# Gated-recurrent stage: the diagonal and the levels of block 1 and 2 in one product per chunk, and narrower stationary operands in the other levels

## The chip, the cores and the metric

The kernel runs on one core of a Trainium2 chip. The time is that of one execution on the device in microseconds; the figure for a kernel is the median of its runs.

## The reference, cut to what matters

The program is a small language model of three blocks on 512 tokens with 1024 channels: a layer of two recurrent mixers, a layer with the gated recurrence of this case (HGRN2), and an attention layer, each with a feed-forward part. Only the second layer's mixer is touched. For each of its 8 heads (128 key and 128 value channels) it computes

```python
# per head
S_t = diag(f_t) S_{t-1} + k_t v_t^T      # k_t = 1 - f_t
o_t = S_t^T q_t
# inside a chunk:
diff = G_[..., :, None, :] - G_[..., None, :, :]          # G = cumsum(log f) in the chunk
pair_decay = jnp.exp(jnp.where(incl, diff, -jnp.inf))     # incl: key s <= query l
attn = jnp.einsum("bhld,bhlsd,bhsd->bhls", q_, pair_decay, k_)
o = einsum(qd_, state) + einsum(attn, v_)
```

The decay differs by channel, so `attn[l, s] = sum_d q[l,d] k[s,d] exp(G[l,d] - G[s,d])` is a matrix product only if the exponent is split into a part for the query and a part for the key.

## The kernel before, in words

Every tensor lies with its channels on the 128 partitions and the 512 tokens along the free dimension, in NT = 4 chunks of P = 128. The five engines run programs of their own, in an order written out by hand, and meet at counting semaphores (`wait_ge`, `then_inc`).

TensorE has two kinds of work in this stage. **Projections**: each head needs four projections (forget, q, gate, v) of 8 groups each, so 32 groups; a group is one `k.product` of three matmuls (L190 to L192, high x high, low x high, high x low) of 128 x 512. They are worked one head ahead and serve as filling: `fill(h, n)` issues the groups between two numbers of `slots_first` (first head, which begins with ten groups), `slots_next`, or, in the last head, `slots_last` (there they are the first products of the output projection, "mix"). **The head's own products** are plain f32, which the profile shows as two passes, two loads and two matmuls, for each product; a transpose has one.

`core(h)` is the order of a head on TensorE. First the diagonal: q against k, 128 x 128 for each of four chunks (L1208); of this the vector engine keeps only the diagonal (`diagonal`, L1493). Then the norm of the head before (L1200), filling, the transposes of v, and seven **levels** l = 0 to 6. A level with block size b = 2^l covers the pairs whose key lies in an even block of b tokens and whose query lies in the odd block behind it. `diff` (VectorE, L1435) subtracts from G its value at the end of the even block, `exps` (ScalarE, L1290 and L1291) takes exponentials of the even and the odd half with opposite signs, `factor` (GpSimd, L1400 and L1401) multiplies k into the even and q into the odd half, giving X, and `level` (TensorE, L1195) multiplies each chunk of X (stationary, 128 columns) with its odd blocks (moving, 64 columns). `merge` (VectorE, L1488) writes the wanted entries into the attention tile with a predicated copy, after it has issued the difference of the level four further on. Behind the levels come the transposes of the decayed keys (L1223), one group of filling, the key-value product (L1229) which waits for ScalarE's copy of the turned keys (`turned_keys`, L1313), filling, the output (L1237 and L1242), and the last filling.

X, the differences and their exponentials have R = 4 buffers, so level l of a head takes the place of level l - 4, and level 0 to 3 of the next head are prepared while the levels of this one are worked. On GpSimd, `step` first makes the decayed keys (L1405) and decayed queries (L1409), then the factors of levels 4 to 6 and of 0 to 3 of the next head.

Of the kernel before, what the change touches and what calls it, by code (L numbers as in the profile page):

```python
# [32 lines left out]
_CST = [("ident", P), ("ones", P), ("upper", P), ("causal", P), ("chunkdiag", P), ("levels", P * len(LEVELS)),  # L33
# [1039 lines left out]
def hgrn2(k, weights, half):  # L1073
# [17 lines left out]
    S = sb("c_S", [P, NT - 1, P], F32)  # L1091
    b_f, b_q, b_g, b_v, b_x0, b_x1, b_kv, b_o = k.ps
# [5 lines left out]
     o_done, osb_ready, osq_ready, nrm_done, rs_ready, y_ready, ch_act, ch_dve) = (sem("c_" + s) for s in (  # L1098
         "f_taken q_taken g_taken raw_ready v_turned v_ready f_clamped sig_ready ft_ready logf_ready q_ready gate_ready g_ready "
         "kdf_ready e_ready kd_ready qd_ready tr_done kdt_ready kv_done s_ready diff_ready lexp_ready x_ready lv_done at_done "  # L1100
         "o_done osb_ready osq_ready nrm_done rs_ready y_ready ch_act ch_dve").split())
# [22 lines left out]
    def odd_mask(l):  # L1124
        b = LEVELS[l]
        m = odd(k.c("levels", l * P, (l + 1) * P), l).rearrange("p (a n) b -> p a n b", a=1)
        return m.to_broadcast([P, NT, P // (2 * b), b]).bitcast(U32)

    def x_at(h, l):
        return NL * h + l + 1  # L1130

# [6 lines left out]
    with nc.Block() as block:  # L1138
# [15 lines left out]
        def _(pe):  # L1154
# [47 lines left out]
            def core(h):  # L1202
                if h == 0:
                    project(1, 0, slots_first[0])
                pe.wait_ge(q_ready, h + 1)
                pe.wait_ge(diff_ready, x_at(h, 0))
                for c in range(NT):
                    ins = nc.tensor.matmul(b_x0[:, c * P:(c + 1) * P], kk[:, c * P:(c + 1) * P], q[:, c * P:(c + 1) * P], start=True, stop=True)  # L1208
                ins.then_inc(lv_done, 1)
# [5 lines left out]
                for l in range(NL):  # L1215
                    level(h, l)
                    fill(h, l + 1)
# [7 lines left out]
                fill(h, 8)  # L1225
# [5 lines left out]
                fill(h, 9)  # L1231
                pe.wait_ge(at_done, 8 * h + 8)
# [11 lines left out]
                fill(h, 10)  # L1244
# [10 lines left out]
        def _(act):  # L1255
# [18 lines left out]
            def silu_q(h):  # L1274
                act.wait_ge(q_taken, h + 1)
                if h:
                    act.wait_ge(lv_done, 8 * (h - 1) + 1)
# [45 lines left out]
            def step(h):  # L1323
# [13 lines left out]
                exps(h + 1, 0)  # L1337
                turned_keys(h)
                high(h + 2, 1)
                exps(h + 1, 1)  # L1340
# [42 lines left out]
            for l in range(R):  # L1383
                exps(0, l)
# [7 lines left out]
        def _(pool):  # L1392
            def factor(h, l):
# [3 lines left out]
                if h0 >= 0:  # L1397
                    pool.wait_ge(lv_done, 8 * h0 + l0 + 2)
# [4 lines left out]
            def step(h):  # L1403
# [8 lines left out]
                if h < H - 1:  # L1412
                    for l in range(R):
                        factor(h + 1, l)

            for l in range(R):
                factor(0, l)
# [6 lines left out]
        def _(dve):  # L1424
            ch = Chain(dve, ch_dve)

            def diff(h, l):
# [7 lines left out]
                nc.vector.tensor_tensor(dif[:, l % R, :].rearrange("p (n b) -> p n b", b=2 * b), g, ref, ALU.subtract).then_inc(diff_ready, 1)  # L1435

# [44 lines left out]
            def merge(h, l):  # L1481
                dve.wait_ge(lv_done, 8 * h + l + 2)
                dve.wait_ge(at_done, 8 * h + l + 1)
                if l + R < NL:
                    diff(h, l + R)
                else:
                    nc.vector.memset(tick[:, l + R - NL:l + R + 1 - NL], 0.0)
                nc.vector.copy_predicated(odd_chunks(at[:, :], l), odd_mask(l), odd_chunks(b_x[(l + 1) % 2][:, :], l)).then_inc(at_done, 1)  # L1488
# [20 lines left out]
            def step(h):  # L1509
                diagonal(h)  # L1510
                merge(h, 0)
                if h:
                    out(h - 1)
                merge(h, 1)
# [10 lines left out]
                diff(h + 1, 0)  # L1525
                merge(h, 6)
                for l in range(1, R):
# [34 lines left out]
            for l in range(R):  # L1562
# [1743 lines left out]
def constants():  # L3306
# [8 lines left out]
        "levels": np.concatenate([(s // (2 * b) == l // (2 * b)) & (s // b % 2 == 0) & (l // b % 2 == 1) for b in LEVELS], 1),  # L3315
        "sel": np.repeat(s == np.arange(6)[None, :], P, 1),
# [106 lines left out]
```

## Time and profile before

| | |
|---|---|
| median of 3 runs | 1744.38 us (1744.16 to 1747.76) |
| the profiled execution, its own time | 1746.02 us |
| its span in the profile | 1744.2 us |
| TensorE matmul row busy | 1697.7 us (97%) |
| TensorE weight loads | 1385.7 us (79%) |
| VectorE | 1071.2 us (61%) |
| ScalarE | 851.9 us (49%) |
| GpSimd | 441.4 us (25%) |

The stage of this case lies between about 763 and 1045 us of the span. Matmuls are pipelined: a record starts when its instruction is taken up and its length holds the time through the array, so records overlap, and what one costs is read from the distance of starts. "PEld" is the row of the weight loads, "PE" that of the matmuls. "128*128" is partitions times columns of the stationary operand, "x8" the number of records merged into a line.

### The profile page before, as it was taken

The numbers are of one execution on the slowest core, as the hardware profiler recorded it, in microseconds if no ns is written. First come the engines' busy times: TensorE is split into PE (matmuls) and PEld (weight loads), VectorE is DVE, ScalarE is ACT, GpSimd is POOL, SyncE is SP. The second block draws the span as 40 slices with busy tenths as digits, with TensorE's granted clock in tenths as the row PEclk, the third lists the DMA queues.
The fourth block names the chain that finished last, engine by engine and source line by source line (L and its number), as shares of the span: only waits on it lengthen the run. The fifth ranks groups of instructions, "written<-read, shape, count | busy, mean of one in ns | idle before, by whom it ended". The sixth has DMA issues, their size and how long they took to land. (4 is left out here: it accounts for less than half of the span.)

```text
span 1744.2 us, 23896 instructions
## 1 busy us (share of the span) xinstructions
PE 1697.7 (97%) x8362; PEld 1385.7 (79%) x8362; DVE 1071.2 (61%) x1684; ACT 851.9 (49%) x1459; POOL 441.4 (25%) x341
## 2 busy tenths in 40 slices
PE   9999999999999999999999999999999999999997
PEld 6787888878888878778888887888887876777785
DVE  6637444377666643587777758766664357888353
ACT  6757545354333332466555645433333244455573
POOL 1445444101111110025654630111111003232232
PEclk9999999999999999999999999999999999999999
DMA  5312112223222232311211212222222232121121
GB/s 220 130 46 73 37 38 67 73 79 109 96 96 96 86 97 96 119 49 61 73 61 61 72 50 85 91 97 96 97 88 97 96 108 101 49 86 60 49 73 48
DMA packets 40372, 144.25 MB, mean 83 GB/s; under 512 B 4562, under 2 KB 4818, under 8 KB 39780
## 3 DMA queue, kind: packets, MB, share of 16 engines
q1 hardware_dynamic: 40292, 143.20, 24.2%
q8 instruction: 49, 0.80, 0.2%
q14 instruction: 31, 0.25, 0.0%
HBM read 141.05 MB, written 2.13 MB: 82 GB/s over the span
## 5 line engine op out<-in xcount | busy, mean ns | idle before, releaser
L190 PE MATMUL bank<-u_high,w_high 128*128 128x512 f32 x1556 | 635.5, 408 | 7.8 <-DVE w_low L582 2.0
L192 PE MATMUL bank<-u_high,w_low 128*128 128x512 f32 x1556 | 609.0, 391 | 0.0
L191 PE MATMUL bank<-u_low,w_high 128*128 128x512 f32 x1556 | 607.4, 390 | 0.0
L190 PEld LDWEIGHTS bank<-u_high,w_high 128*128 128x128 f32 x1556 | 293.0, 188 | 78.6 <-issue 18.9
L192 PEld LDWEIGHTS bank<-u_high,w_low 128*128 128x128 f32 x1556 | 292.4, 188 | 63.5
L191 PEld LDWEIGHTS bank<-u_low,w_high 128*128 128x128 f32 x1556 | 293.3, 188 | 57.9 <-issue 4.1
L154 ACT ACTIVATE w_high<-w_ring 128x1024 fp32r<-128x1024 f32 x228 | 239.2, 1053 | 185.1 <-PE bank L192 160.2
L163 DVE TENSOR_TENSOR w_low<-w_ring,w_high 128x1024 fp32r<-128x1024 f32 x175 | 221.0, 1267 | 159.7 <-ACT w_high L154 159.2
L163 POOL TENSOR_TENSOR w_low<-w_ring,w_high 128x1024 fp32r<-128x1024 f32 x53 | 127.6, 2419 | 333.4 <-ACT w_high L154 333.4
L928 ACT ACTIVATE conv_up<-bank,col_sb 128x512 f32<-128x512 f32 x88 | 68.6, 780 | 263.4 <-DVE bank L988 263.4
L1057 POOL TENSOR_TENSOR hidden<-conv_up 128x512 f32 x44 | 58.3, 1325 | 487.9 <-DVE conv_up L999 364.1
L190 PE MATMUL bank<-src_high_down,w_high 128*128 128x512 f32 x352 | 137.5, 391 | 3.4 <-DVE src_low_down L516 3.4
L988 DVE TENSOR_TENSOR bank<-bank,root_in 128x512 f32<-128x512 f32 x88 | 61.4, 697 | 128.5 <-PE bank L192 126.1
L192 PE MATMUL bank<-src_high_down,w_low 128*128 128x512 f32 x352 | 137.0, 389 | 0.0
L191 PE MATMUL bank<-src_low_down,w_high 128*128 128x512 f32 x352 | 136.9, 389 | 0.0
L1400 POOL TENSOR_TENSOR c_X<-c_k,c_dif 128x256 f32<-128x256 f32 x56 | 58.4, 1042 | 249.6 <-ACT c_dif L1291 249.6
L190 PEld LDWEIGHTS bank<-src_high_down,w_high 128*128 128x128 f32 x352 | 66.1, 188 | 19.4 <-issue 2.2
L192 PEld LDWEIGHTS bank<-src_high_down,w_low 128*128 128x128 f32 x352 | 66.1, 188 | 13.7
L191 PEld LDWEIGHTS bank<-src_low_down,w_high 128*128 128x128 f32 x352 | 66.1, 188 | 13.5
L998 DVE SCALAR_TENSOR_TENSOR conv_up<-bank,col_sb,conv_up 128x511 f32<-128x511 f32 x88 | 65.9, 749 | 17.7 <-ACT conv_up L928 13.5
L999 DVE SCALAR_TENSOR_TENSOR conv_up<-bank,col_sb,conv_up 128x510 f32<-128x510 f32 x88 | 65.9, 748 | 10.1 <-DVE conv_up L998 0.3
L1435 DVE TENSOR_TENSOR c_dif<-c_G 128x512 f32<-128x512 f32 x56 | 54.2, 993 | 24.1 <-PE bank L1195 23.2
(427 smaller groups left out, 2351.9 us busy)
## 6 DMA issues: line engine op xcount, KB each, us to landing
w_ring<-ffn_up SPq DMA_DIRECT2D x88, 512.0 KB, 3.4
w_ring<-ffn_down SPq DMA_DIRECT2D x44, 512.0 KB, 3.4
w_ring<-c_in SPq DMA_DIRECT2D x32, 512.0 KB, 3.5
w_ring<-g_in SPq DMA_DIRECT2D x16, 512.0 KB, 3.5
w_ring<-m_in SPq DMA_DIRECT2D x12, 512.0 KB, 8.1
w_ring<-fox_in SPq DMA_DIRECT2D x12, 512.0 KB, 4.2
w_ring<-dsa_in SPq DMA_DIRECT2D x12, 512.0 KB, 3.4
w_ring<-ab_out SPq DMA_DIRECT2D x8, 512.0 KB, 4.9
```

What stands on the lines that cost most here:

```text
L154: self.nc.scalar.activation(self.ws[s][0][:, :], self.w[:, s, :], ACT.Copy).then_inc(self.w_high, 1)
L163: eng.tensor_tensor(low[:, :], self.w[:, s, :], high[:, :].bitcast(F32), ALU.subtract).then_inc(self.w_split, 1)
L190: nc.tensor.matmul(out, a[0], b[0], start=start, stop=False)
L191: nc.tensor.matmul(out, a[0], b[1], start=False, stop=False)
L192: return nc.tensor.matmul(out, a[1], b[0], start=False, stop=stop)
L928: nc.scalar.activation(cg[:, s, :], bank(i, s)[:, :], ACT.Identity, bias=coef(4 * i + s, 3), scale=coef(4 * i + s, 2)).then_inc(tap_done, 1)
L988: nc.vector.tensor_tensor(bank(i, s)[:, :], bank(i, s)[:, :], k.rn[:, :], ALU.mult).then_inc(taken, 1)
L998: ch.link(nc.vector.scalar_tensor_tensor(cg[:, s, 1:T], bank(i, s)[:, 0:T - 1], coef(4 * i + s, 1), cg[:, s, 1:T], ALU.mult, ALU.add))
L999: nc.vector.scalar_tensor_tensor(cg[:, s, 2:T], bank(i, s)[:, 0:T - 2], coef(4 * i + s, 0), cg[:, s, 2:T], ALU.mult, ALU.add).then_inc(con ...
L1057: nc.gpsimd.tensor_tensor(h[:, bass.ds(2 * i + s // 2, 1), :], cg[:, s - 1:s, :], cg[:, s:s + 1, :], ALU.mult).then_inc(mul_done, 1)
L1400: nc.gpsimd.tensor_tensor(x[:, :, 0, :], blocks(kk[:, :], b)[:, :, 0, :], d[:, :, 0, :], ALU.mult)
L1435: nc.vector.tensor_tensor(dif[:, l % R, :].rearrange("p (n b) -> p n b", b=2 * b), g, ref, ALU.subtract).then_inc(diff_ready, 1)
```

## The change

The diagonal and levels 0 and 1 become one product for each chunk, the near product. It covers groups of four tokens. `near_diff` takes the mean of G at the second and third token of each group as the reference for all four; `near_exps` makes both exponentials of the whole width, `near_factor` multiplies q and k with them over the whole width, and `near` multiplies the two, 128 x 128 for each chunk. `near_merge` copies what the new constant `quad` allows (same group of four, key not later than query) into the attention tile, which GpSimd has set to zero once ahead of the first head. Levels 2 to 6 stay; in each, the last odd block of a chunk can be no key of a pair, so its columns are left out of the stationary operand, and of the output and the merge its partitions: `rows_of(l)` = 124, 120, 112, 96 and 64. The filling is laid out anew: ten numbers in each list in place of twelve. On VectorE the difference of level 4 now follows the near merge directly, and merges 2 and 3 issue those of levels 5 and 6.

```diff
-    slots_first = [10, 12, 14, 16, 18, 20, 22, 24, 26, 27, 29, 32]
-    slots_next = [0, 3, 6, 9, 12, 15, 18, 21, 24, 25, 28, 32]
-    slots_last = [0, 0, 3, 6, 9, 12, 15, 18, 21, 23, 25, 28]
+    slots_first = [10, 13, 16, 19, 22, 24, 26, 28, 30, 32]
+    slots_next = [0, 4, 8, 12, 16, 20, 23, 25, 28, 32]
+    slots_last = [0, 0, 4, 8, 12, 16, 20, 22, 25, 28]
+    NS = NL - 1
...
+    def rows_of(l):
+        return P - LEVELS[l]
+    def step_of(u):
+        return max(u - 1, 0)
+    def used(h, u):
+        return NS * h + step_of(u) + 1
...
+            def near(h):
+                pe.wait_ge(x_ready, x_at(h, 1))
+                for c in range(NT):
+                    s = slice(c * P, (c + 1) * P)
+                    ins = nc.tensor.matmul(b_x0[:, s], X[:, 1, s], X[:, 0, s], start=True, stop=True)
+                ins.then_inc(lv_done, 1)
             def level(h, l):
+                n = step_of(l)
                 pe.wait_ge(x_ready, x_at(h, l))
-                if l >= 1:
-                    pe.wait_ge(at_done, 8 * h + l)
+                if n >= 2:
+                    pe.wait_ge(at_done, NS * h + n - 1)
+                rows = rows_of(l)
                 for c in range(NT):
                     xc = X[:, l % R, c * P:(c + 1) * P]
-                    out = odd(b_x[(l + 1) % 2][:, c * P:(c + 1) * P], l)
-                    ins = nc.tensor.matmul(out, xc, odd(xc, l), start=True, stop=True)
+                    out = odd(b_x[n % 2][0:rows, c * P:(c + 1) * P], l)
+                    ins = nc.tensor.matmul(out, X[:, l % R, c * P:c * P + rows], odd(xc, l), start=True, stop=True)
...
-                pe.wait_ge(q_ready, h + 1)
-                pe.wait_ge(diff_ready, x_at(h, 0))
-                for c in range(NT):
-                    ins = nc.tensor.matmul(b_x0[:, c * P:(c + 1) * P], kk[:, c * P:(c + 1) * P], q[:, c * P:(c + 1) * P], start=True, stop=True)
-                ins.then_inc(lv_done, 1)
+                near(h)
...
-                for l in range(NL):
+                for l in range(2, NL):
                     level(h, l)
-                    fill(h, l + 1)
+                    fill(h, l - 1)
...
+            def near_exps(h):
+                act.wait_ge(diff_ready, x_at(h, 1))
+                nc.scalar.activation(dif[:, 0, :], dif[:, 1, :], ACT.Exp).then_inc(lexp_ready, 1)
+                nc.scalar.activation(dif[:, 1, :], dif[:, 1, :], ACT.Exp, scale=-1.0).then_inc(lexp_ready, 1)
...
+            def near_factor(h, l, x):
+                pool.wait_ge(lexp_ready, x_at(h, l))
+                if h:
+                    pool.wait_ge(lv_done, used(*freed(h, l)))
+                nc.gpsimd.tensor_tensor(X[:, l, :], x[:, :], dif[:, l, :], ALU.mult).then_inc(x_ready, 1)
...
-                    for l in range(R):
+                    near_factor(h + 1, 0, q)
+                    near_factor(h + 1, 1, kk)
+                    for l in range(2, R):
                         factor(h + 1, l)
...
+            nc.gpsimd.memset(at[:, :], 0.0).then_inc(at_zeroed, 1)
...
+            def near_diff(h):
+                g = G[:, :].rearrange("p (n b) -> p n b", b=4)
+                m = mid[:, :].rearrange("p (n b) -> p n b", b=1)
+                ch.link(nc.vector.tensor_tensor(m, g[:, :, 1:2], g[:, :, 2:3], ALU.add))
+                if h:
+                    dve.wait_ge(x_ready, x_at(*freed(h, 1)))
+                nc.vector.scalar_tensor_tensor(dif[:, 1, :].rearrange("p (n b) -> p n b", b=4), m.to_broadcast([P, T // 4, 4]), -0.5, g, ALU.mult, ALU.add).then_inc(diff_ready, 2)
...
             def merge(h, l):
-                dve.wait_ge(lv_done, 8 * h + l + 2)
-                dve.wait_ge(at_done, 8 * h + l + 1)
-                if l + R < NL:
-                    diff(h, l + R)
+                n = step_of(l)
+                dve.wait_ge(lv_done, NS * h + n + 1)
+                dve.wait_ge(at_done, NS * h + n)
+                if l + 3 < NL:
+                    diff(h, l + 3)
...
-            def diagonal(h):
+            def near_merge(h):
                 take(h, 3, vraw, raw_ready)
-                dve.wait_ge(lv_done, 8 * h + 1)
-                nc.vector.tensor_tensor(chunks(at), chunks(b_x0), mask("ident", 0), ALU.mult).then_inc(at_done, 1)
+                dve.wait_ge(lv_done, NS * h + 1)
+                if h == 0:
+                    dve.wait_ge(at_zeroed, 1)
+                nc.vector.copy_predicated(chunks(at), mask("quad", 0).bitcast(U32), chunks(b_x0)).then_inc(at_done, 1)
...
             def step(h):
-                diagonal(h)
-                merge(h, 0)
+                near_merge(h)
+                diff(h, 4)
                 if h:
                     out(h - 1)
-                merge(h, 1)
                 low(h + 1, 3)
                 merge(h, 2)
...
             def last_step(h):
-                diagonal(h)
+                near_merge(h)
+                diff(h, 4)
                 half.low(dve, 0)
-                merge(h, 0)
+                out(h - 1)
                 half.low(dve, 1)
-                out(h - 1)
-                merge(h, 1)
+                merge(h, 2)
                 half.low(dve, 2)
-                merge(h, 2)
                 half.low(dve, 3)
...
+        "quad": (s // 4 == l // 4) & (s <= l),
```

## Rows read from the trace of the kernel before

**Rows 1.** Busy time by stretch, second to last head; columns in the order us, engines, clock.

```profile
801.00:1000.70 199.70, 199.70 (x1136) 170.39 (x1134) 153.19 (x229) 117.75 (x205) 109.51 (x98) 1.00 0.20 66
```

**Rows 2.** TensorE in order of time around one level: start, length, line, form.

```profile
806.39 0.40 PE L191 MATMUL bank<-u_low,w_high 128*128 128x512 f32 x1
...
808.01 0.40 PE L192 MATMUL bank<-u_high,w_low 128*128 128x512 f32 x1
808.25 1.00 PE L1195 MATMUL bank<-c_X 128*128 128x64 f32 x8
...
809.37 0.39 PE L191 MATMUL bank<-u_low,w_high 128*128 128x512 f32 x1
```

**Rows 3.** TensorE in order of time: first products of heads 2 and 8.

```profile
801.01 1.05 PE L1208 MATMUL bank<-c_q,c_k 128*128 128x128 f32 x8
...
1000.70 1.05 PE L1208 MATMUL bank<-c_q,c_k 128*128 128x128 f32 x8
```

**Rows 4.** TensorE in order of time around the key-value product of head 3.

```profile
859.88 0.40 PE L191 MATMUL bank<-u_low,w_high 128*128 128x512 f32 x1
...
860.39 0.94 PE L1229 MATMUL bank<-c_v,c_kdt 128*128 128x128 f32 x6
...
861.40 0.39 PE L191 MATMUL bank<-u_low,w_high 128*128 128x512 f32 x1
```

**Rows 5.** TensorE in order of time, head 1: diagonal product and level 4.

```profile
769.93 1.13 PE L1208 MATMUL bank<-c_q,c_k 128*128 128x128 f32 x8
...
785.60 1.10 PE L1195 MATMUL bank<-c_X 128*128 128x64 f32 x8 [2.44 <-POOL c_X L1401]
```

**Rows 6.** Busy time by stretch, head 1; the third number from the end is TensorE's clock.

```profile
780.00:800.00 20.00, 17.56 (x97) 14.90 (x97) 16.92 (x29) 12.93 (x24) 14.12 (x13) 0.91 0.16 54
```

**Rows 7.** Groups of weight loads over the whole span: busy us, mean ns of one.

```profile
L1195 PEld LDWEIGHTS bank<-c_X 128*128 128x128 f32 x448 | 58.7, 193 | 7.5 <-POOL c_X L1401 3.4
...
L1683 PEld LDWEIGHTS bank<-cst_sb,gate_rows 4*128 4x128 f32 x16 | 1.2, 136 | 0.9 <-issue 0.9
...
L1687 PEld LDWEIGHTS bank<-gate_rows,cst_sb 4*128 4x128 f32 x2 | 0.3, 182 | 0.4 <-DVE gate_rows L2031 0.4
```

**Rows 8.** TensorE in order of time: small transposes of an earlier stage.

```profile
45.61 0.60 PE L1683 MATMUL bank<-cst_sb,gate_rows 4*128 4x4 f32 x8
46.14 0.50 PE L190 MATMUL bank<-u_high,w_high 128*128 128x512 f32 x1
```

**Rows 9.** TensorE in order of time, attention stage: a product of 64 partitions.

```profile
1529.19 0.39 PE L191 MATMUL bank<-u_low,w_high 128*128 128x512 f32 x1
...
1529.65 0.49 PE L3051 MATMUL bank<-cst_sb,a_logits 128*128 128x128 f32 x3
1530.07 0.49 PE L3043 MATMUL bank<-a_k,a_q 64*128 64x128 f32 x4
1530.49 0.94 PE L3064 MATMUL bank<-a_probsT,sq 128*128 128x128 f32 x6
...
1531.50 0.40 PE L191 MATMUL bank<-u_low,w_high 128*128 128x512 f32 x1
```

**Rows 10.** GpSimd in order of time, head 3: factors of level 4 and next level 0.

```profile
842.08 1.18 POOL L1401 TENSOR_TENSOR c_X<-c_q,c_dif 128x256 f32<-128x256 f32 x1
...
859.10 1.33 POOL L1401 TENSOR_TENSOR c_X<-c_q,c_dif 128x256 f32<-128x256 f32 x1
```

**Rows 11.** ScalarE in order of time, start of head 1.

```profile
769.76 1.28 ACT L1382 ACT_TABLE_LOAD   x1
...
773.59 0.61 ACT L1295 ACTIVATE c_kdf<-c_kdf 128x512 f32<-128x512 f32 x1
```

**Rows 12.** Group of GpSimd's full-width products, whole span.

```profile
L1405 POOL TENSOR_TENSOR c_kd<-c_k,c_kdf 128x512 f32<-128x512 f32 x8 | 11.3, 1412 | 0.0
```

**Rows 13.** GpSimd in order of time, start of head 1: first and last of four.

```profile
771.89 1.02 POOL L1400 TENSOR_TENSOR c_X<-c_k,c_dif 128x256 f32<-128x256 f32 x1 [149.96 <-ACT c_dif L1291]
...
774.48 0.89 POOL L1401 TENSOR_TENSOR c_X<-c_q,c_dif 128x256 f32<-128x256 f32 x1
```

More of the change, by code:

```diff
@@ L32 @@
 LEVELS = [1 << n for n in range(7)]
-_CST = [("ident", P), ("ones", P), ("upper", P), ("causal", P), ("chunkdiag", P), ("levels", P * len(LEVELS)),
+_CST = [("ident", P), ("ones", P), ("upper", P), ("causal", P), ("chunkdiag", P), ("levels", P * len(LEVELS)), ("quad", P),
         ("reset", T), ("rcount", 2 * T), ("sel", 6 * P)]
@@ L1091, in hgrn2 @@
     S = sb("c_S", [P, NT - 1, P], F32)
+    mid = sb("c_mid", [P, T // 4], F32)
     b_f, b_q, b_g, b_v, b_x0, b_x1, b_kv, b_o = k.ps
@@ L1097, in hgrn2 @@
      kdf_ready, e_ready, kd_ready, qd_ready, tr_done, kdt_ready, kv_done, s_ready, diff_ready, lexp_ready, x_ready, lv_done, at_done,
-     o_done, osb_ready, osq_ready, nrm_done, rs_ready, y_ready, ch_act, ch_dve) = (sem("c_" + s) for s in (
+     o_done, osb_ready, osq_ready, nrm_done, rs_ready, y_ready, at_zeroed, ch_act, ch_dve) = (sem("c_" + s) for s in (
          "f_taken q_taken g_taken raw_ready v_turned v_ready f_clamped sig_ready ft_ready logf_ready q_ready gate_ready g_ready "
          "kdf_ready e_ready kd_ready qd_ready tr_done kdt_ready kv_done s_ready diff_ready lexp_ready x_ready lv_done at_done "
-         "o_done osb_ready osq_ready nrm_done rs_ready y_ready ch_act ch_dve").split())
+         "o_done osb_ready osq_ready nrm_done rs_ready y_ready at_zeroed ch_act ch_dve").split())
     NL = len(LEVELS)
-    slots_first = [10, 12, 14, 16, 18, 20, 22, 24, 26, 27, 29, 32]
-    slots_next = [0, 3, 6, 9, 12, 15, 18, 21, 24, 25, 28, 32]
-    slots_last = [0, 0, 3, 6, 9, 12, 15, 18, 21, 23, 25, 28]
+    slots_first = [10, 13, 16, 19, 22, 24, 26, 28, 30, 32]
+    slots_next = [0, 4, 8, 12, 16, 20, 23, 25, 28, 32]
+    slots_last = [0, 0, 4, 8, 12, 16, 20, 22, 25, 28]
+    NS = NL - 1
     def chunks(x):
@@ L1122, in odd_chunks, with odd_mask @@
         return x.rearrange("p (c n e b) -> p c n e b", c=NT, e=2, b=b)[:, :, :, 1, :]
-    def odd_mask(l):
+    def odd_mask(l, rows):
         b = LEVELS[l]
-        m = odd(k.c("levels", l * P, (l + 1) * P), l).rearrange("p (a n) b -> p a n b", a=1)
-        return m.to_broadcast([P, NT, P // (2 * b), b]).bitcast(U32)
+        m = odd(k.c("levels", l * P, (l + 1) * P)[0:rows, :], l).rearrange("p (a n) b -> p a n b", a=1)
+        return m.to_broadcast([rows, NT, P // (2 * b), b]).bitcast(U32)
+    def rows_of(l):
+        return P - LEVELS[l]
     def x_at(h, l):
         return NL * h + l + 1
+    def step_of(u):
+        return max(u - 1, 0)
+    def used(h, u):
+        return NS * h + step_of(u) + 1
     def freed(h, l):
@@ L1224, in core @@
                 ins.then_inc(tr_done, 1)
-                fill(h, 8)
+                fill(h, 6)
                 pe.wait_ge(kdt_ready, h + 1)
@@ L1230, in core @@
                 ins.then_inc(kv_done, 1)
-                fill(h, 9)
-                pe.wait_ge(at_done, 8 * h + 8)
+                fill(h, 7)
+                pe.wait_ge(at_done, NS * (h + 1))
                 if h == 0:
@@ L1243, in core @@
                 ins.then_inc(o_done, 1)
-                fill(h, 10)
+                fill(h, 8)
             for h in range(H):
@@ L1276, in silu_q @@
                 if h:
-                    act.wait_ge(lv_done, 8 * (h - 1) + 1)
                     act.wait_ge(x_ready, NL * h)
@@ L1336, in step @@
                 nc.scalar.preload_act_table_set(LNEXP)
-                exps(h + 1, 0)
+                near_exps(h + 1)
                 turned_keys(h)
                 high(h + 2, 1)
-                exps(h + 1, 1)
                 exps(h + 1, 2)
@@ L1382, in _ @@
             nc.scalar.preload_act_table_set(LNEXP)
-            for l in range(R):
+            near_exps(0)
+            for l in range(2, R):
                 exps(0, l)
@@ L1397, in factor @@
                 if h0 >= 0:
-                    pool.wait_ge(lv_done, 8 * h0 + l0 + 2)
+                    pool.wait_ge(lv_done, used(h0, l0))
                 d, x = blocks(dif[:, l % R, :], b), blocks(X[:, l % R, :], b)
@@ L1412, in step @@
                 if h < H - 1:
-                    for l in range(R):
+                    near_factor(h + 1, 0, q)
+                    near_factor(h + 1, 1, kk)
+                    for l in range(2, R):
                         factor(h + 1, l)
-            for l in range(R):
+            nc.gpsimd.memset(at[:, :], 0.0).then_inc(at_zeroed, 1)
+            near_factor(0, 0, q)
+            near_factor(0, 1, kk)
+            for l in range(2, R):
                 factor(0, l)
@@ L1524, in step @@
                 scan(h + 1)
-                diff(h + 1, 0)
+                near_diff(h + 1)
                 merge(h, 6)
-                for l in range(1, R):
+                for l in range(2, R):
                     diff(h + 1, l)
@@ L1561, in _ @@
             scan(0)
-            for l in range(R):
+            near_diff(0)
+            for l in range(2, R):
                 diff(0, l)
```

5 lines of the change are left out of this document (3 added, 2 removed).

## The prediction

> **What bounds the kernel now.** I read the busy time by stretch, the order of time of each engine, and the groups of weight loads. First the busy time of the engines over six heads of the stage: from the second head's start to the last head's, 199.70 us, TensorE's matmul row is busy for all of it at full clock, while VectorE has 153, ScalarE 118 and GpSimd 110 us [rows 1]. A busy matmul row can hide small gaps, so the second view is the order of time, where I compare start distances. Seven high/low projection matmuls take 808.01 - 806.39 = 1.62 us, 0.2314 us each. From one L191 to the L191 behind the next level lie 2.98 us [rows 2]; they hold nine such matmuls (2.08 us), so a level costs 0.90 us. A level is eight f32 passes (two to each of its four chunk products), 0.112 us a pass.
>
> Now count one head by these two prices. 96 projection matmuls are 22.2 us; 84 f32 passes (8 of the diagonal, 56 of the levels, 6 of the state and 14 of the output) are 9.4; seven transposes at the same price 0.8; the norm's two passes, 512 wide and so four times as long, 0.9. That is 33.3 us. The heads of the trace start (1000.70 - 801.01)/6 = 33.28 us apart [rows 3]. So in six heads nothing but TensorE's own instructions makes the time; what leaves TensorE comes off the end, and what leaves the others does not. The one leak that I find is ahead of the key-value product L1229: from L191 at 859.88 to L191 at 861.40 is 1.52 us, of which three projection matmuls and six passes explain 1.37. 0.15 us are lost, where TensorE needs ScalarE's copy of the turned keys [rows 4].
>
> The first head is different. From its diagonal product at 769.93 to the second head's at 801.01 is 31.08 us [rows 3, 5], but by the source it holds only 66 projection matmuls (15.3), the 84 passes (9.4) and seven transposes (0.8), 25.5 us. 5.6 us are lost: one wait of 2.44 us for GpSimd's factor of level 4, smaller ones, and the clock that falls after it. A granted clock of 0.91 over 20 us is 1.8 us of work lost [rows 6].
>
> **What goes, and what it is worth.** Per head two levels go, 16 passes, 16 x 0.112 = 1.79 us of TensorE. The new near product has the form of the old diagonal product (four chunks, 128 columns each way), so it costs the same eight passes and stands in the same place: zero.
>
> **The trimmed stationary operands.** Levels 2 to 6 load 124, 120, 112, 96 and 64 columns in place of 128, 124 of 640 columns fewer. Does a pass get shorter with its load? No stationary operand in this trace is narrower than 128 columns, so the price needs bounds. What sets 0.112 us is the question. It isn't the moving side: a level moves 64 columns and the other f32 products 128, at one price. Nor is it issue: eight transposes of 4 moving columns go from 45.61 to 46.14 us, 0.066 us each [rows 8]. Those load 128 columns too, but in the transposing form, whose load record is 136 ns where the plain one of the same four rows is 182 and a level's 193 [rows 7]. 46 ns shorter load, 46 ns shorter pass: the pass follows the load. If the load goes by columns, a head saves 4.48 x 124/640 = 0.87 us; with level 6 held at the issue distance of about 0.070 us, 0.76. If the chip always loads 128, it saves nothing. One thing may be charged against it. The nearest rows with a narrower array are the attention's products of 64 partitions: from L191 at 1529.19 to 1531.50 are 2.31 us for three projection matmuls (0.69) and 13 passes (1.46); 0.16 us are left over for going into the 64-row shape and back [rows 9]. Level 6 has 64 stationary columns and may pay the same: 0.59 us. I take halfway, 0.67 us a head; ends 0 and 0.87.
>
> The Trainium skill, page "TensorE: Matmul & The Clock Gate", section on LDWEIGHTS, says that a load takes its columns divided by 1.2 GHz, whatever its rows. By that rule a head would save 124/1.2 ns x 8 = 0.83 us. The trace agrees for the full 128 columns (107 ns by the rule, 0.112 us a pass) and shows nothing narrower.
>
> The skill's page "TensorEngine Tiling (Array Packing)", key properties, speaks against the change: a change of tiling mode drains the engine. By it level 6, and no other level, could lose part of what it saves; 0.16 us is what such a change costs here [rows 9].
>
> **Around the levels, in a middle head.** Projection work per level rises from 9 to 12 matmuls and the total stays 96. Two groups in place of one now stand between the key transposes and L1229, so the 0.15 us goes, in the six heads that have it: 0.9 us. VectorE loses two differences, two merges and the diagonal, and gets a midpoint add, one full-width multiply-add and a full-width predicated copy; by the widths less in all. ScalarE trades four half-width exponentials for two full-width ones; GpSimd four half-width products for two full-width. None is the bound, so all of it is worth nothing as long as what they deliver isn't later than TensorE wants it. The tightest: the factor of level 4. It now needs near product, predicated copy, difference 4, ScalarE's value copy and weight split ahead of the exponentials, and GpSimd. In the third head today (start 834.3 by the distance) that factor ends at 842.08 + 1.18 = 843.26, 9.0 us after the start [rows 10]; level 4 will be asked for at 0.90 + 0.85 + 2.78 + 0.45 + two levels with 2.78 us of products each (7.2), less the trims, 12 us. Spare about 3 us: zero cost. Next the following head's near product: today its first factor ends at 859.10 + 1.33 = 860.43 [rows 10], 7.1 us ahead of that head's start (867.6 by the distance); two full-width products in place of two half-width ones take well under 2 us of that: zero.
>
> **The first head** pays for the near product. Its old diagonal product waited only for q and k and ran at 769.93; level 0 came later. Now TensorE has done its ten projection groups by 769.9 and waits at once for both near factors. ScalarE is held by its table load until 769.76 + 1.28 = 771.04, so that the later difference costs nothing; its exponentials are full width, 0.61 us for one such [rows 11]. GpSimd starts at 771.7 and needs two full-width products at 1.41 us [rows 12]: 774.5. Today's four halves for the same number of columns ran from 771.89 to 775.37 [rows 13]. I take 774.9, a wait of 5.0 us, nearly twice that which dropped the clock; so I charge one such drop, 1.8 us. From there the work is 25.5 - 1.79 - 0.67 = 23.0 us: 797.9, plus 1.8 of clock and 1.0 of small waits (the copy of the turned keys stands behind two table loads): 800.7 against 801.01. The other waits of today vanish behind the long one. Worth 0.3 us, not 2.5. Ends: +2.0 with no clock drop, and -2.5 with slow GpSimd and two drops.
>
> **The last head** has no projection group between its first products and level 2; the mixing products behind it want the first low half, which now stands behind the predicated copy and difference 4 on VectorE: 0.3 us lost, by hand.
>
> The constants grow by 128 columns (64 KB), loaded once at the kernel's start: zero.
>
> **The sum.** The seven heads behind the first: 7 x (1.79 + 0.67) = 17.2; turned keys 0.9; first head 0.3; last head -0.3. 18.1 us. The profiled execution took 1746.02 us (span 1744.20, 1.8 around it) and would take 1727.9; the median of the runs is 1744.38, 1.6 lower, so I forecast 1726.3 us.
>
> **Rivals.**
> *Trimmed loads give nothing*, the load being 128 columns wide in any case. For it: all loads of the trace are 128 wide. Then 13.4 us remain: 1731.0. Chance 0.18.
> *Narrow operands cost*: every level of under 128 columns pays the 0.16 us of the 64-row shape [rows 9] and saves nothing. 5 x 8 x 0.16 = 6.4 us more: 1737.4. Against it: 124 or 96 columns fit no smaller shape. Chance 0.06.
> *The long wait comes in every head*: level 4's factor is later than the 3 us spare. Wait alone must eat 2.5 us a head to cancel the gain, 5.5 us beyond today's walk. But past a wait of some 2.5 us the clock falls too, 1.8 us more; a factor 5.5 us late gives 4.3 us a head, 34 us against 18: 1760. Against it: all three helpers get lighter. Chance 0.02.
> *A free first head and full trims*: 12.5 + 6.1 + 0.9 + 2.0 = 21.5 us, 1722.9. Chance 0.10.
> The forecast, with its smaller variants of the first head (1724 to 1730), has 0.64.
>
> **Range and chances.** 1722 to 1733 holds the forecast, the full gain and the loads that give nothing with a poor first head, leaving out the narrow operands that cost and the long waits. What a measurement of this kernel can tell from no change is about 0.2%, 3.5 us. Only the third rival, or a first head and narrow operands that both go wrong, ends above 1741. Faster 0.95, same 0.03, slower 0.02.
>
> **What the profile will show.** Head starts from the second on about 30.7 us apart, TensorE still busy throughout. Eight passes of level 6 within 0.6 us and of level 2 within 0.9; if both are 0.90 apart the first rival is right. Load records of level 6 shorter than 193 ns. Three projection matmuls and L1229's six passes within 1.37 us. A wait of about 5 us ahead of the first near product and half clock behind it. Wrong would be: a distance of 31.5 us (no trim) or over 33 (a wait in each head), or a near product in a middle head that waits for GpSimd.

## The result, and the profile after

The changed kernel takes 1731.94 us (median of four runs, 1730.61 to 1732.98), the kernel before 1745.24 beside it. The ratio is 0.9916 with a 95% interval of 0.9903 to 0.9928: 14.7 us faster (12.6 to 16.9), clear of what a measurement can't tell from no change. Forecast were 18.1 us and 1726.3 us, range 1722 to 1733. Direction and range hold; the likeliest value was 3.4 us too hopeful by the ratio and 5.6 by the medians, and the measured median lies 1.1 us inside the range's upper end.

TensorE in order of time in the changed kernel, from the first near product (L1206) to that of the last head; L1224 is the norm, L1249 the key-value product, L301 the norm of the stage's input, as in the kernel before:

```profile
760.31 1.12 PE L301 MATMUL bank<-root_in,cst_sb 128*128 128x512 f32 x2 [0.85 <-DVE root_in L271]
...
769.62 0.39 PE L191 MATMUL bank<-u_low,w_high 128*128 128x512 f32 x1
774.93 2.07 PE L1206 MATMUL bank<-c_X 128*128 128x128 f32 x8 [4.69 <-POOL c_X L1421]
777.23 0.63 PE L191 MATMUL bank<-u_low,w_high 128*128 128x512 f32 x1
...
797.80 0.94 PE L1249 MATMUL bank<-c_v,c_kdt 128*128 128x128 f32 x6 [1.86 <-ACT c_kdt L1337]
...
802.92 1.05 PE L1206 MATMUL bank<-c_X 128*128 128x128 f32 x8
804.16 1.13 PE L1224 MATMUL bank<-sq,cst_sb 128*128 128x512 f32 x2 [0.19 <-ACT sq L1345]
...
834.22 1.06 PE L1206 MATMUL bank<-c_X 128*128 128x128 f32 x8
...
865.07 1.06 PE L1206 MATMUL bank<-c_X 128*128 128x128 f32 x8
...
988.42 0.83 PE L1206 MATMUL bank<-c_X 128*128 128x128 f32 x6
...
1029.04 0.47 PE L190 MATMUL bank<-u_high,w_high 128*128 128x512 f32 x1 [0.47 <-PEq L1152]
```

Read the starts. From the third head to the last, (988.42 - 834.22)/5 = 30.84 us a head, where [rows 3] gave 33.28. The second takes 31.30. But the first near product stands 14.62 us behind L301 (774.93 - 760.31); the old diagonal product stood 10.04 behind it ([rows 5], and the row below). The matmul at 777.23 is 0.63 us long where it is 0.39 at full clock. Busy time by stretch shows it (the third number from the end is the granted clock as a share of full speed, 2.4 GHz; 0.50 is the lower level, 1.2 GHz):

```profile
802.92:988.42 185.50, 185.31 (x1040) 155.13 (x1039) 135.87 (x212) 115.44 (x195) 103.62 (x87) 1.00 0.22 71
774.90:780.00 5.10, 5.07 (x16) 4.39 (x17) 2.36 (x2) 0.00 (x0) 5.10 (x6) 0.50 0.01 3
...
774.90:785.00 10.10, 10.07 (x47) 8.76 (x48) 4.58 (x4) 2.16 (x4) 7.21 (x8) 0.72 0.01 2
```

In the middle heads TensorE is busy for 185.31 of 185.50 us, the answer to [rows 1]. Over the 10.1 us behind the wait the clock is 0.72, so 2.8 us of work are lost, where [rows 6] gave 1.8. The half clock began while TensorE was still waiting (0.87 over 770.00 to 774.90), and that part of it cost nothing.

Two more rows of the kernel before close the account; they are TensorE's order of time at the stage's two ends, and the changed kernel's rows L301 and 1029.04 above are their counterparts.

```profile
759.89 1.12 PE L301 MATMUL bank<-root_in,cst_sb 128*128 128x512 f32 x2 [0.86 <-DVE root_in L271]
...
1043.64 0.47 PE L190 MATMUL bank<-u_high,w_high 128*128 128x512 f32 x1 [0.47 <-PEq L1138]
```

| stretch of the profiled execution | before | after | difference |
|---|---|---|---|
| start to L301 | 759.89 | 760.31 | +0.42 |
| L301 to the second head's first product | 41.12 | 42.61 | +1.49 |
| second head | 33.33 | 31.30 | -2.03 |
| third to seventh head | 166.36 | 154.20 | -12.16 |
| last head to the matmul behind the stage | 42.94 | 40.62 | -2.32 |
| from there to the end of the span | 700.6 | 702.1 | +1.6 |

The sum is -13.0 us, 1744.2 to 1731.2. The change gives 16.5 us in seven heads and gives 1.5 back in the first; 2.0 are lost outside the stage.

What the narrower operands did is seen in the groups of weight loads of the changed kernel (busy us, mean ns of one):

```profile
L1219 PEld LDWEIGHTS bank<-c_X 128*124 128x124 f32 x64 | 7.6, 188 | 0.0
...
L1219 PEld LDWEIGHTS bank<-c_X 128*112 128x112 f32 x64 | 7.5, 177 | 0.8
L1219 PEld LDWEIGHTS bank<-c_X 128*96 128x96 f32 x64 | 6.7, 164 | 0.9
L1219 PEld LDWEIGHTS bank<-c_X 128*64 128x64 f32 x64 | 4.3, 137 | 2.8 <-issue 2.8
```

A load of 128 columns takes 193 ns [rows 7], one of 64 takes 137: 56 ns for 64 columns, 0.88 ns each. That is close to what the Trainium skill says (page "TensorE: Matmul & The Clock Gate", LDWEIGHTS: columns over 1.2 GHz, 0.83 ns each), and the trace agrees in this cost of a column down to 64 columns, though the record as a whole is longer than its columns over 1.2 GHz. The last line has something that the others lack: 2.8 us in which the load row was idle for "issue", 0.35 us a head.

### The profile page after: what moved, and what is told of

It is laid out like the page before. It is cut to its first block and busy times, and to the rows that moved or that the text cites. A ratio compares the mean times of both kernels' runs of the same rounds, so it can differ in the third digit from the quotient of the medians.

```text
span 1731.2 us, 23547 instructions
## 1 busy us (share of the span) xinstructions
PE 1681.0 (97%) x8234; PEld 1367.4 (79%) x8234; DVE 1047.7 (61%) x1660; ACT 848.1 (49%) x1443; POOL 430.2 (25%) x326
## 5 line engine op out<-in xcount | busy, mean ns | idle before, releaser
L191 PE MATMUL bank<-u_low,w_high 128*128 128x512 f32 x1556 | 608.1, 391 | 0.0
L191 PEld LDWEIGHTS bank<-u_low,w_high 128*128 128x128 f32 x1556 | 293.9, 189 | 58.8 <-issue 4.1
L191 PE MATMUL bank<-src_low_down,w_high 128*128 128x512 f32 x352 | 137.0, 389 | 0.0
L191 PEld LDWEIGHTS bank<-src_low_down,w_high 128*128 128x128 f32 x352 | 66.1, 188 | 13.6
L999 DVE SCALAR_TENSOR_TENSOR conv_up<-bank,col_sb,conv_up 128x510 f32<-128x510 f32 x88 | 65.9, 749 | 10.1 <-DVE conv_up L998 0.3
L2693 DVE TENSOR_TENSOR g_T<-g_T,bank 128x512 f32<-128x512 f32 (+1 forms) x48 | 30.7, 643 | 50.5 <-PE bank L2268 50.4
L1430 POOL TENSOR_TENSOR c_X<-c_k,c_dif 128x256 f32<-128x256 f32 x40 | 40.1, 1002 | 54.6 <-ACT c_dif L1315 54.4
```

The costliest lines, as they stand in the source:

```text
L191: nc.tensor.matmul(out, a[0], b[1], start=False, stop=False)
L999: nc.vector.scalar_tensor_tensor(cg[:, s, 2:T], bank(i, s)[:, 0:T - 2], coef(4 * i + s, 0), cg[:, s, 2:T], ALU.mult, ALU.add).then_inc(con ...
L1430: nc.gpsimd.tensor_tensor(x[:, :, 0, :], blocks(kk[:, :], b)[:, :, 0, :], d[:, :, 0, :], ALU.mult)
L2693: nc.vector.tensor_tensor(t, t, z, ALU.subtract).then_inc(t_ready, 1)
```

## The experiments

Executions of one kernel lie up to 6.5 us apart (1744.68 to 1751.14 for the kernel before, beside the run with the longer first filling), so small effects are read from start distances in the traces. From the third head on these repeat within 0.03 us in the changed kernel and within 0.12 in the kernel before. "Third head" below is the distance from L301 to the third head's first product; it is 74.45 us before and 73.91 after (834.22 - 760.31). This one repeats less well: a second profile of the changed kernel, the first run below, has 73.51, so a difference of 0.4 us in it says nothing.

**The changed kernel again.** No edit. The 1.6 us behind the stage had two readings: the clock fell there once more than in the kernel before, for a reason outside the change, or the change has slowed that part.

> The changed kernel as it is, beside the others on one chip. [...]

Measured: 1731.49 us, ratio 0.9912 (0.9897 to 0.9927). The part behind the stage is 702.1 us again, with a clock of 0.96 over the index stage of the attention, as in the first profile; the kernel before has 1.00 there:

```profile
1445.00:1485.00 40.00, 38.76 (x174) 26.53 (x173) 29.93 (x45) 17.73 (x33) 24.19 (x14) 0.96 0.22 80
```

By this run alone the second reading would stand. The later runs decide it: level 6 with 72 columns and the longer first filling have 700.5 us behind the stage, all 128 columns and the early copy 702.1 and 702.0, the trim alone, all three edits and the last two versions 703.6, and none of them edits anything there. The clock over 1445 to 1485 us in the run of all three edits:

```profile
1445.00:1485.00 40.00, 38.75 (x159) 25.97 (x157) 30.70 (x45) 15.23 (x29) 20.30 (x13) 0.91 0.18 74
```

The steps are 1.6 us: none, one or two stretches of half clock. The trim alone has two without any near product; so the loss isn't tied to the near product, and it isn't a slower stage. What picks the number stays open. The changed kernel had one in both profiles, but the clock is not fixed by the kernel: the five executions with the longer first filling took 1725.74 to 1729.76 us at mean clocks of 0.999 to 0.996.

This run also shows how the first head varies. Its near product starts 14.60 us behind L301, and this is the clock behind it:

```profile
772.95:785.00 12.05, 12.05 (x61) 10.49 (x62) 6.90 (x8) 3.83 (x7) 9.31 (x10) 0.81 0.14 45
```

2.3 us are lost here, 2.8 in the first profile; the half clock covered more of the wait and less of the work. That is about the 0.4 us between the two third-head distances.

**All 128 stationary columns.** The moving side and the merges stay as in the change.

```diff
-                    out = odd(b_x[n % 2][0:rows, c * P:(c + 1) * P], l)
-                    ins = nc.tensor.matmul(out, X[:, l % R, c * P:c * P + rows], odd(xc, l), start=True, stop=True)
+                    out = odd(b_x[n % 2][:, c * P:(c + 1) * P], l)
+                    ins = nc.tensor.matmul(out, xc, odd(xc, l), start=True, stop=True)
```

> The changed kernel with all 128 stationary columns loaded in every level and the merges still narrow. Theory A (the trims are worth what the start distances of the trace say, 0.48 us a head): head starts 31.3 us apart in place of 30.8, 3.9 us slower than the changed kernel. Rival B (the trims are worth nothing and the near product gives it all): no difference. Rival C (they are worth the 0.87 us a head of the load going by columns alone): 6.9 us slower.

Measured: 1734.02 us, ratio 0.9927 (0.9913 to 0.9941). Two successive heads:

```profile
832.88 1.06 PE L1206 MATMUL bank<-c_X 128*128 128x128 f32 x8
864.13 1.06 PE L1206 MATMUL bank<-c_X 128*128 128x128 f32 x8
```

31.26 us a head over five heads (31.25 for the two shown); the trims are worth 0.42 us a head, 3.4 in all, and the near product 33.28 - 31.26 = 2.02. In time the run is 2.5 us slower than the changed kernel beside it (1731.49). Theory A holds in kind and is 0.06 us high in size. Rivals B and C fall: the trims do give something, half of what the load by columns alone would.

**72 columns in level 6.** Eight more columns are loaded than the change loads; the merge takes 64 as before.

```diff
-                rows = rows_of(l)
+                rows = max(rows_of(l), 72)
```

> The changed kernel, with 72 stationary columns in level 6 in place of 64; the eight more are loaded and never merged. Theory A (at 64 columns the product takes a narrower array shape, and going into it and out of it costs about 0.24 us): eight passes of level 6 in about 0.56 us in place of 0.80, head starts 30.6 us apart, 1.9 us faster than the changed kernel. Rival B (a pass has a floor of about 0.1 us for another reason, so 64 columns cannot be faster): the distance stays or grows by 0.05 us a head.

Measured: 1728.23 us, ratio 0.9900 (0.9885 to 0.9916). TensorE in order of time in this run, around level 6 of one head:

```profile
850.41 0.39 PE L191 MATMUL bank<-u_low,w_high 128*128 128x512 f32 x1
850.87 0.67 PE L1219 MATMUL bank<-c_X 128*72 128x64 f32 x8
851.67 0.39 PE L191 MATMUL bank<-u_low,w_high 128*128 128x512 f32 x1
```

And the same place in the changed kernel:

```profile
852.94 0.39 PE L191 MATMUL bank<-u_low,w_high 128*128 128x512 f32 x1
853.48 0.68 PE L1219 MATMUL bank<-c_X 128*64 128x64 f32 x8
854.42 0.39 PE L191 MATMUL bank<-u_low,w_high 128*128 128x512 f32 x1
```

The stretch holds three projection matmuls (0.69 us) and eight passes. With 72 columns it is 1.26 us, with 64 it is 1.48. Of the 0.22 us between them 0.08 lie ahead of the first pass (0.46 us after L191 with 72 columns, 0.54 with 64) and 0.14 from there to the next L191 (0.80 against 0.94). The head distance falls from 30.84 to 30.60 us. A load that is eight columns longer makes the head 0.24 us shorter, which only something at 64 columns itself can do; rival B falls. In time the run is 3.3 us faster than the changed kernel beside it, but 1.6 of that is the index stage.

Where the 0.24 us lie can be read too. The last line of each block merges passes six to eight of level 6, the changed kernel first:

```profile
852.94 0.19 PEld L192 LDWEIGHTS bank<-u_high,w_low 128*128 128x128 f32 x1
853.48 0.54 PEld L1219 LDWEIGHTS bank<-c_X 128*64 128x64 f32 x8 [0.35 <-issue]
853.82 0.34 PE L1219 MATMUL bank<-c_X 128*64 128x64 f32 x3
```

```profile
850.42 0.19 PEld L192 LDWEIGHTS bank<-u_high,w_low 128*128 128x128 f32 x1
850.64 0.76 PEld L1219 LDWEIGHTS bank<-c_X 128*72 128x72 f32 x8
851.18 0.36 PE L1219 MATMUL bank<-c_X 128*72 128x64 f32 x3
```

With 64 columns the first load starts 0.54 us behind the load before it, with 72 only 0.22. Inside the group the narrower passes are the quicker ones: 58 ns from start to start against 65. So the price isn't paid for each pass; it is paid on going in and on coming out. The load row's idle time for level 6 falls with it, from 2.8 to 1.0 us, which is what the lines of 96 and 112 columns have (mean load 144 ns):

```profile
L1219 PEld LDWEIGHTS bank<-c_X 128*72 128x72 f32 x64 | 5.4, 144 | 1.0
```

This is the rule that spoke against the change: the Trainium skill, page "TensorEngine Tiling (Array Packing)", key properties, has a change of tiling mode drain the engine. The trace agrees in that a level of 64 columns costs 0.24 us more than one of 72, while the levels of 72, 96, 112 and 120 columns save what their columns are worth within 0.06 us; that it is a drain is the page's word, the runs show its price and its place.

**The trims without the near product.** The kernel before, with `rows = P - LEVELS[l]` in all seven levels and merges; the matmul is shown, its output, mask and merge are narrowed in the same way.

```diff
-                    ins = nc.tensor.matmul(out, xc, odd(xc, l), start=True, stop=True)
+                    ins = nc.tensor.matmul(out, X[:, l % R, c * P:c * P + rows], odd(xc, l), start=True, stop=True)
```

> The kernel before with the trimmed stationary operands alone: all seven levels and the diagonal product stay, levels 0 and 1 load 127 and 126 columns. Theory A (trim and near product are independent, and the losses at the first head belong to the near product): head starts 32.8 us apart in place of 33.28, 3.9 us faster than the kernel before, the first head's diagonal product still 10.0 us behind the norm product L301 and the wait of some 2.4 us for level 4's factor still there. Rival B (they add up otherwise): anything else between 0 and 7 us faster.

Measured: 1742.92 us, ratio 0.9982 (0.9973 to 0.9992). TensorE in order of time:

```profile
758.63 1.13 PE L301 MATMUL bank<-root_in,cst_sb 128*128 128x512 f32 x2 [0.85 <-DVE root_in L271]
...
768.66 1.13 PE L1209 MATMUL bank<-c_q,c_k 128*128 128x128 f32 x8
...
784.31 1.00 PE L1196 MATMUL bank<-c_X 128*112 128x64 f32 x8 [2.52 <-POOL c_X L1402]
...
832.13 1.05 PE L1209 MATMUL bank<-c_q,c_k 128*128 128x128 f32 x8
864.99 1.05 PE L1209 MATMUL bank<-c_q,c_k 128*128 128x128 f32 x8
```

Heads 32.85 us apart over five heads: the trims give 0.43 us here too, so they and the near product add up (0.43 + 2.02 = 2.45 of the 2.44 measured). The diagonal product is again 10.03 us behind L301: the later start of the first head belongs to the near product. The wait for level 4's factor is there, at 2.52 us. In time this run is 3.1 us faster by the ratio where 3.9 were expected, with 3.1 us of half clock in the index stage of its profile against it. Theory A.

**More filling ahead of the first near product.**

```diff
-    slots_first = [10, 13, 16, 19, 22, 24, 26, 28, 30, 32]
+    slots_first = [16, 16, 19, 22, 24, 26, 28, 30, 31, 32]
```

> The changed kernel with another list of projection groups for the first head only: 16 of the 32 groups stand ahead of the first near product in place of 10 (slots_first = 16, 16, 19, 22, 24, 26, 28, 30, 31, 32). Theory A (the near product waits for GpSimd's two factors whatever TensorE does, so work put ahead of it is free): the wait of 4.7 us ahead of the first near product shrinks below 1 us, the two half-speed windows behind it go (3.4 us), the second head starts 36 to 38 us after the norm product L301 in place of 42.6, and smaller waits for level 4's factor and the turned keys appear; 4 to 6 us faster than the changed kernel. Rival B (the wait only moves: the chain through GpSimd, ScalarE and VectorE of the first head sets when the second starts): the second head starts within 1 us of 42.6.

Measured: 1729.34 us, ratio 0.9891 (0.9876 to 0.9907). Its waits, and the clock from the first of them to 20 us behind the long one:

```profile
772.35 1.16 PE L1206 MATMUL bank<-c_X 128*128 128x128 f32 x8 [0.65 <-POOL c_X L1421]
...
780.88 1.00 PE L1219 MATMUL bank<-c_X 128*112 128x64 f32 x8 [1.06 <-POOL c_X L1431]
...
792.06 0.94 PE L1249 MATMUL bank<-c_v,c_kdt 128*128 128x128 f32 x6 [2.71 <-ACT c_kdt L1337]
...
798.42 1.12 PE L1224 MATMUL bank<-sq,cst_sb 128*128 128x512 f32 x2 [1.24 <-ACT sq L1345]
```

```profile
772.00:812.00 40.00, 34.57 (x204) 28.71 (x205) 33.82 (x47) 25.21 (x45) 29.20 (x27) 1.00 0.22 67
```

The near product starts at the same distance from L301 as before (14.64 us): it does wait for GpSimd whatever TensorE does. The wait shrinks from 4.69 to 0.65 us, the clock stays full, and the second head starts 38.4 us behind L301 in place of 42.6. Of these 4.2 us 1.1 are lost in the second head (32.36 us), which now waits 1.24 us for the square of the first head's output. Rival B falls. Theory A has the mechanism and is too hopeful: 38.4 lies outside its 36 to 38 us, 3.1 us come through at the third head (2.7 against the second profile) where 4 to 6 were expected, and the clock gave back 2.8 us at most, not 3.4. By the ratios this run is 3.7 to 4.4 us faster. The profiled execution was the quickest of the five (1725.74 us); that the clock stays full in this stage doesn't hang on it, since the profiles of the two later versions with the same list also have 1.00 over 772 to 812 us.

**Early copy of the turned keys, first head.**

```diff
                 silu_q(h + 1)
+                if h == 0:
+                    turned_keys(h)
                 silu_gate(h)
                 nc.scalar.preload_act_table_set(LNEXP)
                 near_exps(h + 1)
-                turned_keys(h)
+                if h:
+                    turned_keys(h)
```

> The changed kernel where, in the first head only, ScalarE copies the turned keys ahead of the gate's silu and of the table load, not behind both and the next head's near exponentials. Theory A (the key-value product of the first head waits for that copy alone): the wait of 1.86 us goes and the second head starts 2 us earlier, 40.6 us after L301; 2 us faster than the changed kernel. Rival B (behind it the output or the next near product waits as long for something else): less than 0.5 us of the 2 comes through.

Measured: 1730.18 us, ratio 0.9901 (0.9886 to 0.9915). The wait at L1249 is gone and the second head starts 40.4 us behind L301. But this is the second head:

```profile
798.83 1.05 PE L1206 MATMUL bank<-c_X 128*128 128x128 f32 x8
...
801.40 1.12 PE L1224 MATMUL bank<-sq,cst_sb 128*128 128x512 f32 x2 [1.52 <-ACT sq L1345]
...
831.43 1.06 PE L1206 MATMUL bank<-c_X 128*128 128x128 f32 x8
```

It takes 32.60 us, the third starts 73.04 us behind L301 against 73.91 (73.51 in the second profile). Of 2.2 us 0.9 come through, 0.5 by the second profile. Theory A is right on the second head and not on the time, rival B names the wrong product; the wait moved to the norm product, for which ScalarE is late by its own work: from the copy of the turned keys at 792.57 to the end of the square at 801.35 it has no wait that the trace lists.

**All three edits** (16 groups first, early copy, 72 columns).

> The changed kernel with all three edits: 16 groups ahead of the first near product, the early copy of the turned keys in the first head, and 72 stationary columns in level 6. Theory A (the three are independent): head starts 30.60 us apart, second head 35 to 38 us after L301, 7 to 9 us faster than the changed kernel, some 1723 us. Rival B (with the first head's bare wait gone the chain of the helpers is the bound there, so the early copy adds nothing to the new list): 5 to 6 us.

Measured: 1726.95 us, ratio 0.9878 (0.9861 to 0.9895). Second head at 36.88 us behind L301, third at 69.45, heads 30.60 apart, and two waits:

```profile
794.70 0.49 PE L1262 MATMUL bank<-c_qd,c_S 128*128 128x128 f32 x2 [1.32 <-DVE c_S L1552]
...
799.58 0.70 PE L1224 MATMUL bank<-sq,cst_sb 128*128 128x512 f32 x1 [1.61 <-ACT sq L1345]
```

By the traces 4.5 us from L301 to the third head and 0.24 in each of six later ones, 5.9 us; in time 5 us by the median and 5.9 to 6.6 by the ratios, nearer to rival B. But the early copy adds 1.3 us to the new list at the second head (36.88 against 38.42, less the 0.24 us of the 72 columns), so B's reason is wrong. What is missing is lost in the first head, where the output now waits 1.32 us for VectorE's state, and at L1224.

**The norm product of the second head behind its filling**, once on the early copy alone and once on all three.

```diff
-                if h:
+                if h > 1:
                     norm(h - 1)
                 fill(h, 0)
+                if h == 1:
+                    norm(h - 1)
```

> The early copy of the turned keys in the first head, and in the second head alone the norm product of the head before stands behind the four projection groups, not ahead of them. Theory A (what the early copy gained in the first head was lost in the second, where TensorE now waited 1.52 us for the square of the first head's output ahead of L1224, and nothing else was late): that wait goes, the second head takes 30.8 us in place of 32.6, and the third starts 71.3 us behind L301 in place of 73.0. Rival B (the norm's result is then late for the gated output or for the key transposes, and the wait comes back later in the second head): the third head starts within 0.5 us of 73.0.

> All of it: 16 groups ahead of the first near product, the early copy, 72 stationary columns in level 6, and the norm product of the second head behind its filling. Theory A: the third head starts 67.9 us behind L301 in place of 69.45, the wait of 1.61 us at L1224 goes, every later head 30.60 us; some 1.6 us faster than without the moved norm. Rival B as in the other run: no gain.

Measured: 1729.86 us, ratio 0.9911 (0.9894 to 0.9927), and 1724.71 us, ratio 0.9876 (0.9860 to 0.9893). In the first of the two no wait is left in the second head, it takes 30.85 us and the third starts 71.15 us behind L301 (73.04 without). In the second:

```profile
758.45 1.13 PE L301 MATMUL bank<-root_in,cst_sb 128*128 128x512 f32 x2 [0.83 <-DVE root_in L271]
...
795.34 1.16 PE L1206 MATMUL bank<-c_X 128*128 128x128 f32 x8
799.09 1.02 PE L1224 MATMUL bank<-sq,cst_sb 128*128 128x512 f32 x2
...
826.05 1.06 PE L1206 MATMUL bank<-c_X 128*128 128x128 f32 x8
```

67.60 us to the third head, against 69.45 and, in the change itself, 73.91. Theory A holds in both by the start distances, which is where the moved norm is seen; the ratios alone don't show it (0.9911 against 0.9901 without it, 0.9876 against 0.9878), and the first of the two has 1.6 us more of half clock behind the stage than the run that it is set against. This last version beats both kernels; from the start distances it gains 6.3 us in the first two heads and 0.24 us in each of six more, 7.7 us on the changed kernel. The medians give 7.2, the ratios 6.3 to 7.0.

## Why the prediction was right, and where its terms were off

*What bounds the kernel.* Right. TensorE is busy 185.31 of 185.50 us in six heads, and what was taken off it came off the end: 2.02 us a head by the near product and 0.42 by the trims are the 2.44 by which the head starts moved together.

*The near product.* 1.94 us a middle head was forecast (two levels 1.79, the copy of the turned keys 0.15); 2.02 us is what full columns show. The 0.15 us ahead of L1249 has gone, as read.

*The trims.* Forecast 0.67 us a head, halfway between 0.76 and 0.59; measured 0.42 and 0.43. The argument (a pass follows its load, a load follows its columns) is right in kind: by start distances level 5, with 96 columns, saves 0.19 us where columns alone give 0.22, and level 3, with 120, 0.06 for 0.06. The term that was too small is the price of the 64-column shape: taken at half of 0.16 us from the 64-partition rows, it is 0.24, so level 6 gave 0.10 us where the sum had 0.26, and its eight passes took 0.79 us and not the 0.6 that the profile was to show. That is 0.16 of the missing 0.25 us. The other 0.09 are missing in levels 2 to 5: columns alone give 0.42, their own start distances add up to about 0.37, the head shows 0.32, and why is open. Over seven heads the 0.25 us are 1.7, the largest error inside the steady part, of which the near product made good 0.5. The rival "trimmed loads give nothing" is refuted, and of "narrow operands cost" only level 6 is true.

*The first head.* Forecast 0.3 us gained, measured 1.5 lost. The wait was right: the near product was put at 15.0 us behind L301 and stands at 14.6. Off were the clock behind it (1.8 us charged, 2.8 lost) and the copy of the turned keys (1.0 for all small waits, 1.86 for this one). With enough work ahead of the near product both clock and wait go. The price of a fall of the clock was tied to the length of the wait (one of some 2.5 us lets it fall); the runs don't bear that out, as the last section shows.

*A cost that I had missed.* The second head waits for ScalarE's square of the first head's output (0.19 us in the trace) and takes 31.30 in place of 30.84 us; with the norm product moved behind the filling it takes 30.85. It is the next late thing in line, and grows to 1.5 us as soon as the first head gets shorter.

*The last head.* 0.3 us of loss was charged; it is 2.32 us shorter where the others are 2.44, so 0.1.

*Outside the stage.* 2.0 us of the difference between the two profiles lie there, 1.6 in a clock that was lower in the index stage. That was in no term, and the runs don't lay it to the change.

*The sum.* Forecast: 18.1 us in seven heads, 0.3 gained in the first, 0.3 lost in the last, 18.1 in all. Measured: 16.5 in the seven heads with the last one's loss in it, where that makes 17.8 forecast (1.3 less); 1.5 lost in the first head (1.8 less); 2.0 lost outside the stage. 18.1 - 1.3 - 1.8 - 2.0 = 13.0, the difference of the spans.

*What the time alone could not tell.* The rival "trimmed loads give nothing" stood at 1731.0 us, nearer to the measured 1731.94 than the forecast's 1726.3. It is refuted by the start distances of two runs, not by the time; losses in the first head and in the index stage happened to bring the median to its place.

## What to carry to other kernels

Where TensorE's matmul row is full and the distances between groups are explained by its own instructions, price a removed product by start distances, not by the length of its record; this came out within 0.1 us a head. Look separately at the ends of such a stage: a product that is merged with others waits for the latest of their inputs, and in the first head too little work stood in front of it. And columns left out of an f32 stationary operand shortened each pass at every width that was run (124 down to 72), while 64 cost 0.24 us for each group of eight passes between 128-wide products; widths from 65 to 71 and below 64 were not run.

## What the runs showed that I had not expected

A product of 72 stationary columns is faster than one of 64: 1.26 us against 1.48 for the same stretch.

TensorE's waits don't tell its clock by their length alone. A wait of 2.44 us was followed by half clock in the kernel before; in the run with the longer first filling one of 2.71 us was not (0.65 and 1.06 us ahead of it), and the clock was 1.00 over that whole stretch and the 20 us behind it. The wait of 4.69 us in the changed kernel cost 2.8 us of work in one profile and 2.3 in the other. The same untouched index stage ran with a clock of 1.00, 0.96 or 0.91 over 40 us in different kernels.
